# Four places instead of three for rounded weight units, with a smaller DMA scratch for GpSimd

## The reference

```
mod = silu(c) @ ada_w[l] + ada_b[l]            # 1024 -> 6 * 1024
h = rms_norm(x, g_pre_mix[l]) * (1 + scale_m) + shift_m
q, k, v, u = split(h @ w_in[l] + b_in[l])
mix = concat(window_attention(rotary(q), rotary(k), v, sinks), causal_pool(u) ) @ w_out[l]
x = x + gate_m * rms_norm(mix, g_post_mix[l])
h = rms_norm(x, g_pre_ffn[l]) * (1 + scale_f) + shift_f
x = x + gate_f * rms_norm((silu(h @ w_gate[l]) * (h @ w_up[l])) @ w_down[l], g_post_ffn[l])
```

## Time and profile before

| | us |
|---|---|
| median of 3 runs (lowest, highest) | 1228.93 (1228.01, 1229.20) |
| the profiled execution, its own time | 1232.94 |
| its span, first to last instruction | 1230.1 |
| PE busy in the span | 1155.8 (94%) |
| DVE busy | 822.9 (67%) |
| ACT busy | 636.1 (52%) |
| mean granted clock of PE, share of full | 0.985 |

### The profile page before, as it was taken

How to read it: one execution, slowest core, us unless ns; L and a number is a source line. 1 busy time by engine, 2 the same in 40 slices (tenths; PEclk the granted TensorE clock), 3 DMA queues, 4 the chain that set the end, 5 groups by cost and what they waited for, 6 DMA issues and landing times.

```text
span 1230.1 us, 19723 instructions
## 1 busy us (share of the span) xinstructions
PE 1155.8 (94%) x7931; PEld 1041.9 (85%) x7931; DVE 822.9 (67%) x1273; ACT 636.1 (52%) x1106; POOL 43.9 (4%) x73
## 2 busy tenths in 40 slices
PE   5859899999888899999999999999999999999998
PEld 3448899999776799999898789999989878999996
DVE  5797877796794565555658567565666856756564
ACT  3154643444644743434655666454556566645454
POOL 2200000000200100000000000000000000000000
PEclk9979999999999999999999999999999999999999
DMA  9967599998461275667353245555545423555540
GB/s 377 404 227 309 206 277 314 308 394 311 160 258 51 103 289 209 238 190 274 119 181 139 102 160 198 200 190 189 188 144 180 141 99 138 190 201 192 190 153 34
DMA packets 37305, 252.97 MB, mean 206 GB/s; under 512 B 4416, under 2 KB 4704, under 8 KB 8928
## 3 DMA queue, kind: packets, MB, share of 16 engines
q1 hardware_dynamic: 34992, 244.47, 55.9%
q0 software_dynamic: 2080, 7.25, 1.6%
q10 hardware_dynamic: 144, 0.00, 0.0%
HBM read 250.64 MB, written 1.06 MB: 205 GB/s over the span
## 4 chain that ended last, share of the span: by engine, by line
PE 81%; DVE 10%; ACT 4%; DMA 3%; issue 2%; SPq 0%; DVEq 0%; ACTq 0%
PE bank L479 25%; PE bank L481 25%; PE bank L480 25%; DMA raw_w<-weights 3%; PE bank L486 3%; DVE lo_w L1439 2%; DVE raw_w L1449 2%; ACT gtok L1096 1%; PE bank L595 1%; PE bank L526 1%; DVE prob L1558 1%; ACT hi_w L1090 1%; DVE smax L1561 1%; PE bank L872 1%; DVE normed L1519 1%
## 5 line engine op out<-in xcount | busy, mean ns | idle before, releaser
L1439 DVE TENSOR_TENSOR lo_w<-raw_w,hi_w 128x1024 fp32r<-128x1024 f32 (+2 forms) x354 | 420.7, 1209 | 147.1 <-ACT hi_w L1090 146.4
L1090 ACT ACTIVATE hi_w<-raw_w 128x1024 fp32r<-128x1024 f32 (+2 forms) x354 | 359.7, 1040 | 188.7 <-PE bank L481 96.4
L479 PE MATMUL bank<-in_hi,lo_w 128*128 128x256 f32 x1408 | 395.8, 281 | 0.0
L480 PE MATMUL bank<-in_lo,hi_w 128*128 128x256 f32 x1408 | 392.9, 279 | 0.0
L481 PE MATMUL bank<-in_hi,hi_w 128*128 128x256 f32 x1408 | 392.8, 279 | 0.0
L479 PEld LDWEIGHTS bank<-in_hi,lo_w 128*128 128x128 f32 x1408 | 264.3, 188 | 2.6 <-issue 0.8
L480 PEld LDWEIGHTS bank<-in_lo,hi_w 128*128 128x128 f32 x1408 | 263.6, 187 | 1.9 <-issue 0.5
L481 PEld LDWEIGHTS bank<-in_hi,hi_w 128*128 128x128 f32 x1408 | 264.7, 188 | 0.0
L479 PE MATMUL bank<-hi_w,in_lo 128*128 128x256 f32 (+2 forms) x496 | 158.7, 320 | 18.6 <-DVE in_lo L1540 12.5
L480 PE MATMUL bank<-lo_w,in_hi 128*128 128x256 f32 (+2 forms) x496 | 155.9, 314 | 0.0
L481 PE MATMUL bank<-hi_w,in_hi 128*128 128x256 f32 (+2 forms) x496 | 155.5, 313 | 0.0
(11 more groups left out here) (208 smaller groups left out, 1069.0 us busy)
## 6 DMA issues: line engine op xcount, KB each, us to landing
raw_w<-weights SPq DMA_DIRECT2D x219, 1024.0 KB, 4.9
ink<-ink_w SPq DMA_DIRECT2D x8, 640.0 KB, 13.3
rows<-norm_rows POOLq DMA_DIRECT2D x5, 512.0 KB, 4.7
rows<-mod_rows POOLq DMA_DIRECT2D x4, 512.0 KB, 9.2
raw_w<-weights SPq DMA_DIRECT2D x2, 832.0 KB, 4.2
const<-const_table SPq DMA_DIRECT2D x1, 1538.0 KB, 9.4
raw_w<-weights SPq DMA_DIRECT2D x2, 768.0 KB, 4.4
shared<-bias_rows POOLq DMA_DIRECT2D x2, 640.0 KB, 8.2
```

What stands on the lines that cost most here:

```text
L479: nc.tensor.matmul(o, st[1], mv[0], start=start, stop=False, **kw)
L480: nc.tensor.matmul(o, st[0], mv[1], start=False, stop=False, **kw)
L1090: nc.scalar.activation(hi_w[:, m % NSPLIT, cut], raw_view(unit)[:, cut], ACT.Identity).then_inc(*sig("hi_w", unit, i))
L1439: nc.vector.tensor_tensor(lo_w[:, m % NSPLIT, cut], raw_view(unit)[:, cut], hi_w[:, m % NSPLIT, cut].bitcast(F32), ALU.subtract).then_inc( ...
```

## The change

`hi_w` and `lo_w` get four places (`NSPLIT` = 4), 16 KB more of each SBUF partition, and the compiler's front end is told to keep 2048 bytes of each partition for the descriptors of GpSimd's DMAs. Unit m goes to place m mod 4 and waits for the unit four numbers back. ACT and DVE make every unit ready one unit earlier in their lists: `("gu", L, 1)` at the end of the mixer instead of in the first chain, units p + 4 instead of p + 3 in the feed forward, and `("in", 1, 3)` or `("gqk", L, 0)` in the last chain of the block before instead of in the mixer. `behind` moves with the unit that it belongs to. SP's and PE's lists stay as they are.

```diff
-NSPLIT = 3
+NSPLIT = 4
...
# ACT, prepare(unit)
-                if m < NSPLIT:
+                if m < 3:
                     sc.wait_ge(*due("ink_used", (1, 3, 3)[m]))
-                else:
+                if m >= NSPLIT:
                     sc.wait_ge(*due(*counts.last_use.get(SPLITS[m - NSPLIT], ("none",))))
...
# DVE, lo(unit)
-                if m < NSPLIT:
+                if m < 3:
                     ve.wait_ge(*(due("ink_used", 5) if m == 0 else due("in", 0, 1, 2)))
...
# attention_windowed(L), ACT (the same two edits on DVE with lo and behind)
                 if L == 1:
-                    prepare(("in", 1, 3))
                     prepare(("in", 1, 4))
...
                 prepare(("gu", L, 0))
+                prepare(("gu", L, 1))
...
# attention_mixed(L), ACT (the same on DVE with lo)
-                prepare(("gqk", L, 0))
...
                 prepare(("gu", L, 0))
+                prepare(("gu", L, 1))
...
# feed_forward(L), ACT (the same on DVE with lo and behind)
-                    prepare(units[3 + T])
+                    prepare(units[4 + T])
...
-                    nxt = units[p + 3] if p + 3 < len(units) else None
+                    nxt = units[p + 4] if p + 4 < len(units) else None
...
# ACT and DVE
-            following = {L: [("in", 1, i) for i in range(3)] if L == 0 else [("z", L + 1, i) for i in range(3)] if L + 1 < NL else [] for L in range(NL)}
+            following = {L: [("in", 1, i) for i in range(4)] if L == 0 else [("z", L + 1, i) for i in range(3)] + [("gqk", L + 1, 0)] if L + 1 < NL else []
+                         for L in range(NL)}
...
-                    chain(L, 0, T, ("gu", L, 1 + T))
+                    chain(L, 0, T, ("gu", L, 2 + T))
...
-                    chain(L, 1, T, following[L][1 + T] if L + 1 < NL else None)
+                    chain(L, 1, T, following[L][2 + T] if L + 1 < NL else None)
...
-        nc = bacc.Bacc("TRN2", target_bir_lowering=False, num_devices=1)
+        nc = bacc.Bacc("TRN2", target_bir_lowering=False, num_devices=1, dynamic_dma_scratch_size=2048)
```

More of the change, by code:

```diff
@@ L1655, in attention_windowed @@
                     evacuate(1, 1, 0)
-                    lo(("in", 1, 3))
-                    behind(("in", 1, 3))
                     lo(("in", 1, 4))
@@ L1706, in attention_windowed @@
                 lo(("gu", L, 0))
+                lo(("gu", L, 1))
             def attention_mixed(L):
@@ L1739, in turned @@
                     last.then_inc(*sig("kr2", L, T, frees=("cT", L, T, 1)))
-                lo(("gqk", L, 0))
                 lo(("rqk", L, 0))
@@ L1837, in feed_forward @@
                 for T in range(2):
-                    lo(units[3 + T])
-                    behind(units[3 + T])
+                    lo(units[4 + T])
+                    behind(units[4 + T])
                 def convolve(f):
```

## The result

| | before | after |
|---|---|---|
| median | 1229.55 us (20 runs, 1226.41 to 1238.31) | 1235.97 us (20 runs, 1227.77 to 1238.15) |
| ratio of the paired comparison | | 1.0035, 95% interval 1.0021 to 1.0049 |
| the profiled execution, its own time / span | 1232.94 / 1230.1 | 1231.82 / 1229.7 |

The change makes the kernel slower, by 0.35%, which is 4.3 us (2.6 to 6.0). The forecast was +4.0. The profiled execution of the changed kernel is the third quickest of its 20, so the two spans show no loss; the stages have to be compared one by one.

What follows compares the result with a forecast made beforehand. PE was taken to bound the kernel, busy 1155.8 of 1230.1 us. Block 0's delays 4.5, clock 1.2, block 1's mixer -1.4 and blocks 2 and 3 -0.3 sum to +4.0: 1232.9 us, range 1226.5 to 1237.5.

Steps and rivals of the forecast that it cites:

- step 3: PE's clock falls behind a 3.6 us gap ahead of block 0's T = 1 transposes: +1.2 us, bounds 0 and 2.4.
- step 4: Block 1's mixer: T = 1 2.3 us late, then DVE has 4.6 less; ACT's rounding limits the gain to -1.4 us.
- Step 1: Into block 0's feed forward, T = 0: the new remainder pair ahead of `gained` is not hidden, +2.2 us.
- Step 2: Between block 0's chains of T = 0 and T = 1: modulation unit ("ada", 0, 20) now goes first, +2.3 us.
- Step 5: Blocks 2 and 3: `gqk` leaves the mixer, about -0.15 us each, -0.3; extra `gu` pair at mixers' end costs 0.
- Step 6: The rest: units p + 4, loads asked for one unit sooner and GpSimd's smaller scratch cost 0; scratch bounds 0 and 5 us.
- A: Rival, 25%: bare delays, clock does not fall or one block 0 delay is hidden; 1230.8 without the fall, down to 1228.5.
- B: Rival, 12%: the mixers are DVE's, so what DVE sheds in blocks 1 to 3 counts in full; -4.7 us, 1224.2.
- C: Rival, 8%: GpSimd's queue stalls or loads come late in block 0's feed forward; some 5 us on top, 1238.

Runs made afterwards that it cites:

- e4: Changed kernel with block 0's entry as before: remainder pair back in T = 0's chain, modulation unit behind T = 1; 0.9987 against the kernel before.
- e6: Kernel before with block 0's modulation units one place sooner, so that one stands between the chains of T = 0 and T = 1; 1.0028.
- e2: Changed kernel with block 0's modulation unit ("ada", 0, 20) back behind the chain of T = 1; 1.0014 against the kernel before.
- e5: Changed kernel with block 1's modulation units later: 12 behind T = 1's chain, 13 in the mixer, 14 and 15 behind the softmax; 1.0009 against before.
- e7: Changed kernel with 14 useless PE transposes ahead of T = 1's transposes in blocks 0 and 1; 1.0010 against the kernel before.
- e8: Changed kernel with block 0's entry as before and block 1's modulation units late, e4 and e5 in one; 0.9969 against the kernel before.
- e10: Kernel before with only the smaller scratch of GpSimd's DMAs, a repeat of e1; 1.0004.
- e11: Kernel before (three places, old scratch) with block 1's modulation units 14 and 15 moved behind the softmax; 0.9958, 1223.73 us against 1230.09.
- e3: Changed kernel with the remainder pair back in block 0's T = 0 chain, a modulation unit still between the chains; 1.0032 against the kernel before.
- e1: Kernel before with only the smaller scratch of GpSimd's DMAs (2048 bytes); 1.0017.

## Why the prediction was right, and where it was not

**The sum** was right: +4.0 forecast, +4.3 measured, and on the median that I started from the ratio gives 1228.93 x 1.0035 = 1233.2 against 1232.9. (The two medians above lie 6.4 apart, a little more than the interval of the ratio allows.) The two largest terms held; the others were off in ways that cancelled. e4 splits the sum in two: block 0's entry 5.9 against 4.5 + 1.2 = 5.7, the rest -1.6 against -1.7. Inside these halves the agreement is in part luck: the clock fell elsewhere than forecast (step 3), and the rest is stages c, d and f, where c gave less than forecast and d gave what was not forecast at all (step 4).

**Step 1, the pair ahead of `gained`: right.** Forecast +2.2. From ACT's last `in_hi` to `normed` of T = 0: before 122.73 - 106.14 = 16.59, after 121.22 - 102.49 = 18.73, so +2.14; e4, without the pair, 16.59. That `rows` would follow the pair instead of covering it was the reading that mattered: an idle time of 3.34 us in front of `normed` was no slack, since what ended it hung on the same chain.

**Step 2, the unit between the chains: right.** Forecast +2.3. Alone in the kernel before (e6) +2.29. Together with the pair stage a grew by 4.24 against 4.5.

**Step 3, the clock: a cost of about the right size, from another place.** I expected a gap of 3.6 us ahead of T = 1's transposes and the fall behind it, and named that gap as what would show me right. The gap was 1.11 us. The clock had already fallen one chain sooner: the pair made PE's gap ahead of T = 0's transposes 2.82 us, before 0.68, the front of T = 0 ran at 0.50 and so filled the time that DVE's modulation unit took. Step 1 brought its own fall, which I had not thought of: in all four profiles with the pair in that place (after, e2, e5, e7) the front of T = 0 ran at half clock, of the ten without it in three (e8, e10, e11), and there for a shorter time. A second fall at the start of the feed forward then cost 1.6 (stage b against e7, which has the first fall and not the second), against the 1.2 of the sum, and e7 got 3.1 us back by keeping PE at work. And the fall is no fixed price: in e5 the same list escaped the second one, and in e3 it lay in full in the feed forward, where b is 4.0 above the 179.36 of before, 0.6 of it the wait for a remainder. So one execution can lose more in one fall than the 2.4 that I took as the bound for two; as a mean, 5.9 (e4 against the changed kernel) less 4.2 (stage a) leaves 1.7 for the clock in block 0.

The mechanism as I wrote it does exist where the pair is not in its way. In e6 and e3 the gap was 3.54 us and the clock fell behind it, in e6 for +1.21 us, the 1.2 of the sum. And in block 1 of the changed kernel, where nothing was added ahead of T = 0's `gained`, it is there too:

```profile
331.28 1.78 PE L526 MATMUL bank<-const,normed 128*128 128x128 f32 x8 [3.54 <-DVE normed L1520]
333.77 0.55 PE L479 MATMUL bank<-hi_w,in_lo 128*128 128x256 f32 x1 [0.71 <-DVE in_lo L1541]
```

What I overlooked is how steps 1 and 2 act together: the first delay's fall slows the work that stands ahead of the second gap, and so closes it.

The Trainium skill, "TensorE: Matmul & The Clock Gate", Part 1, has the default throttled and an idle PE falling back to half rate. The traces agree: the front behind the idle 2.82 us ran at 0.50. They also show two executions of one list of which one fell at 138 and the other did not.

**Step 4, block 1's mixer: the mechanism right, the size 0.6 off as a mean, and a gain behind it missed.** Forecast -1.4, with ACT's rounding of `("wo", 1, 3)` as the limit. Measured -0.91 in stage c, with ACT's rounding as the limit (0.42 us). But single profiles lead astray here: with the list of before c was 45.42, 45.37 (e6), 44.01 and 44.21 (e1, e10, whose clock held on the front of T = 1), with the changed list 44.51, 43.76, 43.86 and 43.72 (e2 to e4). The means are 44.75 and 43.96, -0.8. In all four profiles of the changed list the clock fell at the front of T = 1; against the two of the old list in which it fell too (before, from which I forecast, and e6, mean 45.40) the gain is the 1.4 of the forecast. The extra -1.5 of stage d I did not forecast. The window of the kernel before in which its output projection begins:

```profile
378.00:380.00 2.00, 2.00 (x6) 1.54 (x5) 0.00 (x0) 0.54 (x2) 0.00 (x0) 0.50 0.00 0
```

And the like one of the changed kernel:

```profile
379.00:381.00 2.00, 2.00 (x10) 1.61 (x9) 0.57 (x1) 2.00 (x3) 0.00 (x0) 1.00 0.00 0
```

The kernel before runs it at 0.50 of the clock for a while, in each of before, e1, e6 and e10 (d 53.4 to 53.5), and the four kernels with the changed list (after, e2, e3, e4, d 51.9) do not. Ahead of the projection PE waited 1.54, 2.09, 0.56 and 1.33 us for DVE before, and 0.56, 1.05 and 0.47 after. That this is why the clock held is my reading; no run isolates it. It does not need the fourth place: e11, with three, has gaps of 0.36, 1.05 and 0.62 there and the same d of 51.94.

**Step 5: right.** Stage f is -0.36 in the kernels with the changed list (e7: -0.29), against about -0.3 for two such blocks together, so the term is 0.4 short at most. The moved `("gqk", L, 0)` cost nothing: DVE idles 7.28 us where its pair stood. The pair at the mixer's end in block 1 cost nothing either.

**Step 6: right as far as it can be told** (e1, e10). The loads that a fourth place asks for sooner helped nobody, since PE waits 1.6 us for them before and after.

**The rivals.** A, the bare delays without a fall of the clock, is what e7 comes near to: 1228.93 x 1.0010 = 1230.2, against 1230.8 of the rival. So the clock is what set the forecast apart from it, as the forecast said, though e7's interval (1228.3 to 1231.9) is wide. B, that the mixers are DVE's, was the rival with more truth than its chance: taken alone, units out of block 1's mixer are worth 5 us (e11). In block 2 its condition did not hold (f -0.36, not -2). The change only got little of it since it put one of them between the chains, where it costs as much as it saves. C was not seen in the changed kernel. In e1, e3 and e4 PE waited 0.4 to 0.6 us for a remainder in block 0's feed forward; the other eleven profiles, seven of them with the small scratch, have no such wait, so nothing follows from it.

## What to carry to other kernels

A deeper ring moves every later instruction of its lists one unit forward, and what stands at a stage's edge is then a new instruction in a chain where all wait for one another. Read the lists at those edges first, and ask of each idle time whether what ends it hangs on the chain itself, for then it is no cover. And try the moved work without the resource: two units placed behind the softmax gave 0.42% with three places, where the change with its fourth place cost 0.35%.

## What was not expected of the hardware

Executions of one kernel differ by as much as an edit is worth, and where two profiles of one list could be compared, most of the difference was a stretch at 0.50 of the clock more or fewer. Between profiles of the list of before, stage c runs from 44.0 to 45.4 (e1, without a fall in it, and before, with one), and the start from 103.6 to 106.1 (e10, with a clock of 0.92 over its first 102.4 us, and before, with 0.90). Not all is the clock: stage b runs from 179.0 to 180.1 (e10, e1) though neither has a fall in it, and 0.6 of that is e1's wait for a remainder. The mean granted clock of the changed kernel's 20 runs went from 0.979 to 0.986. Over all runs it was 0.982 in the changed kernel and 0.986 to 0.987 in the kernel before. Useless transposes in a gap of PE were worth 3 us (1.0035 to 1.0010).
